# Rounding pieces of W_out earlier and reordering the end of an attention loop

## The chip, the cores and the metric

The kernel runs on one core of a Trainium2 chip. The metric is the device time of one execution, in microseconds (us). Five engines work side by side, each through its own list of instructions in order: TensorE (PE) multiplies and transposes, VectorE (DVE), ScalarE (ACT) and GpSimd (POOL) work elementwise, and SyncE (SP) issues DMAs. They wait for one another through semaphores only.

## The reference

Two layers of an encoder on 1024 tokens of 1024 features, in float32. Each layer mixes tokens with three kinds of heads (neighbourhood attention, a gated unit, a Fourier transform), normalises every head, multiplies by `w_out`, and then applies a SwiGLU block:

```
for l in range(DEPTH):                       # DEPTH = 2
    h = rms_norm(x, norm_mix_g[l])
    q, k, v, z_b, x_c = jnp.split(h @ w_in[l], splits, axis=-1)
    mix_a = neighbourhood_attention(q, k, v, rpb[l])
    mix_b = spatial_gating(z_b, ...)
    mix_c = fourier_mix(x_c)
    mix = head_rms_norm(jnp.concatenate([mix_a, mix_b, mix_c], axis=-1), head_norm_g[l])
    x = x + mix @ w_out[l]
    h = rms_norm(x, norm_ffn_g[l])
    x = x + (jax.nn.silu(h @ w_gate[l]) * (h @ w_up[l])) @ w_down[l]
return rms_norm(x, final_norm_g)
```

## The kernel before

Every float32 product is made of three products of rounded halves (`split3`, L1647): an operand is split into a rounded part "hi" (ACT, a copy to the rounded type) and the remainder "lo" (DVE or POOL, a subtraction), and hi*hi, hi*lo and lo*hi are summed in a PSUM bank. All activations are kept transposed, features on the 128 partitions.

The order of work is written out by hand on every engine, with `l` as the layer. What matters here is the attention loop and the stage after it.

The attention loop works through 8 tiles of 128 queries, each with 8 heads, two heads in each of 32 steps `i`. On PE a step is `scores(i)` (L1773, six matmuls on L1786), `values(i - 2)` (L1804, twelve on L1819), and two `turn_probs` (L1793, six transposes on L1800). DVE adds the bias and takes the maximum (L1243), ACT takes the exponent (`probs`, L864, L868), and the turned probabilities are copied from PSUM by DVE (L1253) for even heads and by ACT (L880) for odd ones. When a tile's values are done, DVE copies them to SBUF (`att_heads`, L1266), PE turns them to tokens (`turn_heads`, L1826, L1834), ACT squares (L892), DVE sums (L1281, L1285), POOL raises to the power -1/2 (L652), DVE multiplies (`att_tok`, L1290), PE turns them back (`turn_tokens`, L1837, L1841), and ACT copies them to `att_raw` (L897). The banks are shared: 6 and 7 take the turned tiles by parity, and in the first eight steps also the batches of the other heads (`turn_batch`, L1846), whose halves ACT (L887) and DVE (L1258) make. `turn_heads(0)` waits for the batch before last, since it takes over its bank.

The output product of the stage after the loop needs `w_out` in 16 pieces, numbered 18 to 33, each 128 x 1024. SP loads a piece (L435) as soon as its place in SBUF is free, ACT makes its hi part (`piece_hi`, L699, L702) and POOL its lo part (`piece_lo`, L620, L624). Where in its list ACT takes a piece is given by the step: 18 at step 14, 19 at 29, 20 at 33, 21 at 36. On POOL, piece 18 stands behind the power of tile 2, 19 behind that of tile 5, 20 behind that of tile 6, and the rest behind that of tile 7. Pieces 18, 19 and 20 belong to features of the other heads, whose input is ready long before, so PE begins the output product with them while the last tile is still on its way: `out_early(b)` (L1867) is 9 matmuls into bank b, three with each of the three pieces, and each bank waits until the attention loop is done with it. Between the eight `out_early` calls PE turns the last tiles. Pieces 21 to 25 follow in order, 24 matmuls each, and then the second half of the tokens with pieces 26 to 33.

Of the kernel before, what the change touches and what calls it, by code (L numbers as in the profile page):

```python
# [151 lines left out]
def build(nc, x, win, wout, wom, wg, wu, wd, bias, wsp, bsp, lng, lnb, gmix, ghead, gffn, gfin,  # L152
          tw, bd, ident, out):
    ctx = ExitStack()
    with ctx:
# [457 lines left out]
        @block.gpsimd  # L613
        def _(pool):
            nc.gpsimd.memset(ONES[:, :], 1.0).then_inc(memsets, 1)
            nc.gpsimd.memset(NHALF[:, :], -0.5).then_inc(memsets, 1)
            nc.gpsimd.memset(EPS_T[:, :], EPS).then_inc(memsets, 1)
            pool.wait_ge(memsets, 3)

            def piece_lo(l, p):  # L620

                s = ALL_SLOT[p]
                pool.wait_ge(w_hi, split_nth(l, p))
                nc.gpsimd.tensor_tensor(WL[s][:, :], WR[s][:, :], WH[s][:, :], ALU.subtract).then_inc(w_ready, 1)  # L624

            def ffn_rstd(n):

                pool.wait_ge(y_var, n)
                nc.gpsimd.tensor_tensor(RTF[:, :], RTF[:, :], NHALF[:, 0:4], ALU.pow).then_inc(y_rstd, 1)

            pool.wait_ge(w_ready, 1)
            piece_lo(0, 1)
            for l in range(DEPTH):
                piece_lo(l, 2)
                pool.wait_ge(rt_var, l + 1)
                nc.gpsimd.tensor_tensor(RT[:, :], RT[:, :], NHALF[:, 0:8], ALU.pow).then_inc(rt_made, 1)
                for p in (3, 4, 5, 6, 7, 8):
                    piece_lo(l, p)
                pool.wait_ge(ln_var, l + 1)
                nc.gpsimd.tensor_tensor(LR[:, :], LR[:, :], NHALF[:, 0:8], ALU.pow).then_inc(ln_rstd, 1)  # L640
                for p in (14, 15, 9, 10, 12, 11):
                    piece_lo(l, p)
                for n in range(2):
                    pool.wait_ge(hs_var, l * 2 + n + 1)
                    nc.gpsimd.tensor_tensor(SR[:, :], SS[:, :], NHALF[:, :], ALU.pow).then_inc(hs_rstd, 1)
                    if n == 0:
                        piece_lo(l, 13)
                for p in (17, 16):
                    piece_lo(l, p)
                for t in range(8):  # L650
                    pool.wait_ge(o_var, l * 8 + t + 1)
                    nc.gpsimd.tensor_tensor(SR[:, 0:HA], SS[:, 0:HA], NHALF[:, 0:HA], ALU.pow).then_inc(o_rstd, 1)  # L652
                    if t in (2, 5, 6):
                        piece_lo(l, {2: 18, 5: 19, 6: 20}[t])
                for p in range(21, 30):
                    piece_lo(l, p)
                ffn_rstd(2 * l + 1)
                for p in range(30, PIECES):
                    piece_lo(l, p)
                ffn_rstd(2 * l + 2)  # L660
                if l + 1 < DEPTH:
                    piece_lo(l + 1, 0)
                    pool.wait_ge(t_lo, (l + 1) * DN_STEPS)
                    piece_lo(l + 1, 1)
            for h in range(2):
                ffn_rstd(2 * DEPTH + h + 1)
# [3 lines left out]
        def _(act):  # L670
# [28 lines left out]
            def piece_hi(l, p):  # L699
                s = ALL_SLOT[p]  # L700
                act.wait_ge(w_landed[s], 16 * (l * PER_SLOT[s] + nth_in_slot(p) + 1))
                nc.scalar.activation(WH[s][:, :], WR[s][:, :], ACT.Copy).then_inc(w_hi, 1)  # L702
# [95 lines left out]
            for l in range(DEPTH):  # L798
# [73 lines left out]
                for i in range(41):  # L872
                    if i < 32:
                        probs(2 * i)
                    if 1 <= i < 33:
                        t = 2 * (i - 1) + 1
# [6 lines left out]
                    if i < 8:  # L883
                        b = BATCHES[i]
# [9 lines left out]
                    if i >= 12 and i % 4 == 0:  # L894
# [2 lines left out]
                        nc.scalar.activation(raw_out(tile),  # L897
                                             B[6 + tile % 2][:, :].rearrange("p (k r c) -> p k r c", k=NP, c=QC),
                                             ACT.Copy).then_inc(raw_made, 1)
                    if i in (14, 29, 33):  # L900
                        piece_hi(l, {14: 18, 29: 19, 33: 20}[i])
                    if i == 36:
                        mixed_hi(0)
                        piece_hi(l, 21)
                for p in range(22, 26):
                    piece_hi(l, p)
                mixed_hi(1)
                piece_hi(l, 26)
# [58 lines left out]
                for r in range(DN_STEPS):  # L967
# [8 lines left out]
                    i = r - 58  # L976
# [649 lines left out]
        def _(pe):  # L1626
# [26 lines left out]
            for l in range(DEPTH):  # L1653
# [9 lines left out]
                for k in range(KT_D):  # L1663
                    p = k // 4
# [219 lines left out]
                for i in range(33):  # L1884
                    if i < 32:
                        scores(i)
                    if i >= 2:
                        values(i - 2)
                    if i >= 10 and i % 4 == 2:
                        turn_tokens((i - 10) // 4)  # L1890
                    if i >= 1:
                        turn_probs(2 * (i - 1))
                        turn_probs(2 * (i - 1) + 1)
                    if i < 8:
                        turn_batch(i)
                    if i >= 7 and i % 4 == 3:
                        turn_heads((i - 7) // 4)
                pe.wait_ge(bt_lo, l * 8 + 8)
                out_early(0)
                values(31)  # L1900
                turn_tokens(6)
                out_early(1)
                turn_heads(7)
                for b in (2, 3, 4):
                    out_early(b)
                turn_tokens(7)
                for b in (6, 5, 7):
                    out_early(b)
# [195 lines left out]
```

## Time and profile before

| | us |
|---|---|
| median of 3 runs | 2129.43 |
| lowest and highest | 2127.15, 2131.02 |
| the profiled execution | 2130.46 |
| its span | 2128.7 |

| engine | busy us | share of the span |
|---|---|---|
| PE | 2077.0 | 98% |
| DVE | 1455.3 | 68% |
| ACT | 837.4 | 39% |
| POOL | 237.4 | 11% |

The span is the profiled stretch of that execution; 1.8 us lie around it. Busy times of an engine are summed over its instructions. The mean of the TensorE clock granted over the span was 0.994 of full speed.

### The profile page before, as it was taken

How to read it: one execution, taken by the hardware profiler on the slowest of the kernel's cores; microseconds unless marked ns; L12 is line 12 of the kernel's file. 1: busy time of each engine (PE TensorE's matmuls, PEld its weight loads, DVE VectorE, ACT ScalarE, POOL GpSimd, SP SyncE). 2: the span in 40 equal slices, each digit the busy share in tenths (PEclk: the TensorE clock that was granted, in tenths of full speed). 3: DMA queues.
4: the chain of work that ended last, by engine and by line, in shares of the span. 5: the costliest groups of instructions: out<-in, count | busy, mean ns of one | idle time of the engine just before them, and what ended most of it. 6: DMA issues, size and time to landing. Idle time of an engine off the chain costs nothing.

```text
span 2128.7 us, 27845 instructions
## 1 busy us (share of the span) xinstructions
PE 2077.0 (98%) x10352; PEld 1711.6 (80%) x10352; DVE 1455.3 (68%) x2355; ACT 837.4 (39%) x1476; POOL 237.4 (11%) x104
## 2 busy tenths in 40 slices
PE   7999999999999999999999999999999999999997
PEld 6888777887888888888888887787788888878886
DVE  6414684789877777787843237657997777777876
ACT  5221573453333323444622217634433332334442
POOL 2223024300000000000023300242000000000000
PEclk9999999999999999999999999999999999999998
DMA  5122343314333326633221314431253333384333
GB/s 182 60 89 70 119 120 109 99 45 157 116 102 102 104 99 227 222 98 96 85 78 60 97 43 139 140 131 38 69 173 103 101 104 99 114 285 131 96 97 114
DMA packets 104790, 240.21 MB, mean 113 GB/s; under 512 B 11088, under 2 KB 14032, under 8 KB 104400
## 3 DMA queue, kind: packets, MB, share of 16 engines
q1 hardware_dynamic: 92032, 211.16, 30.9%
q10 hardware_dynamic: 12624, 27.26, 3.6%
q8 instruction: 84, 1.38, 0.3%
q14 instruction: 50, 0.41, 0.1%
HBM read 188.58 MB, written 49.81 MB: 112 GB/s over the span
## 4 chain that ended last, share of the span: by engine, by line
PE 86%; DVE 7%; issue 3%; ACT 2%; DMA 1%; POOL 1%; DVEq 0%; POOLq 0%; SPq 0%; ACTq 0%
PE bank L1649 25%; PE bank L1651 25%; PE bank L1650 25%; PE bank L1819 2%; PE bank L1786 2%; PE bank L1800 2%; DVE s_lo L1083 1%; DVE t_lo L1332 1%; PE bank L1735 1%; DMA t_raw<-hidden_b 1%; DVE x_res L1300 1%; DVE y_sq_sum L1312 1%; PE bank L1737 0%; ACT y_sq L777 0%; PE bank L1841 0%
## 5 line engine op out<-in xcount | busy, mean ns | idle before, releaser
L1649 PE MATMUL bank<-t_hi,s_hi 128*128 128x512 f32 x1320 | 514.9, 390 | 10.3 <-DVE hid_g L1446 6.7
L1651 PE MATMUL bank<-t_hi,s_lo 128*128 128x512 f32 x1320 | 513.6, 389 | 0.0
L1650 PE MATMUL bank<-t_lo,s_hi 128*128 128x512 f32 x1320 | 513.6, 389 | 0.0
L1649 PEld LDWEIGHTS bank<-t_hi,s_hi 128*128 128x128 f32 x1320 | 247.8, 188 | 65.5 <-DVE hid_g L1446 9.2
L1651 PEld LDWEIGHTS bank<-t_hi,s_lo 128*128 128x128 f32 x1320 | 247.8, 188 | 51.4
L1650 PEld LDWEIGHTS bank<-t_lo,s_hi 128*128 128x128 f32 x1320 | 247.8, 188 | 51.3
L624 POOL TENSOR_TENSOR w_lo<-w_raw,w_hi 128x1024 fp32r<-128x1024 f32 x67 | 176.9, 2649 | 948.4 <-ACT w_hi L702 836.7
L1649 PE MATMUL bank<-h_hi,w_hi 128*128 128x512 f32 x512 | 202.1, 395 | 7.6 <-POOL w_lo L624 7.6
L1649 PE MATMUL bank<-b_hi,s_hi 128*128 128x512 f32 x528 | 206.6, 391 | 0.1
L1651 PE MATMUL bank<-b_hi,s_lo 128*128 128x512 f32 x528 | 206.2, 390 | 0.0
L1650 PE MATMUL bank<-b_lo,s_hi 128*128 128x512 f32 x528 | 206.0, 390 | 0.0
L1650 PE MATMUL bank<-h_lo,w_hi 128*128 128x512 f32 x512 | 200.2, 391 | 0.0
L1651 PE MATMUL bank<-h_hi,w_lo 128*128 128x512 f32 x512 | 200.2, 391 | 0.0
L734 ACT ACTIVATE s_hi<-w_u 128x512 fp32r<-128x512 f32 x146 | 92.2, 631 | 233.8 <-PE bank L1651 196.4
L734 ACT ACTIVATE s_hi<-w_down 128x512 fp32r<-128x512 f32 x154 | 97.2, 631 | 186.8 <-PE bank L1651 186.1
L1083 DVE TENSOR_TENSOR s_lo<-w_down,s_hi 128x512 fp32r<-128x512 f32 x154 | 107.4, 698 | 71.4 <-ACT s_hi L734 71.4
L734 ACT ACTIVATE s_hi<-w_g 128x512 fp32r<-128x512 f32 x146 | 92.0, 630 | 159.7 <-PE bank L1651 116.7
L1649 PE MATMUL bank<-w_hi,h_hi 128*128 128x512 f32 (+1 forms) x384 | 137.3, 358 | 13.5 <-DVE h_lo L1003 13.5
L1650 PE MATMUL bank<-w_lo,h_hi 128*128 128x512 f32 (+1 forms) x384 | 136.5, 356 | 0.0
L1651 PE MATMUL bank<-w_hi,h_lo 128*128 128x512 f32 (+1 forms) x384 | 136.5, 355 | 0.0
L702 ACT ACTIVATE w_hi<-w_raw 128x1024 fp32r<-128x1024 f32 x68 | 70.7, 1057 | 137.8 <-DMA w_raw<-in_win 116.7
L1649 PEld LDWEIGHTS bank<-h_hi,w_hi 128*128 128x128 f32 x512 | 96.6, 189 | 28.6 <-POOL w_lo L624 8.5
(196 smaller groups left out, 3274.7 us busy)
## 6 DMA issues: line engine op xcount, KB each, us to landing
w_g<-in_wg SPq DMA_DIRECT2D x44, 512.0 KB, 3.6
w_u<-in_wu SPq DMA_DIRECT2D x44, 512.0 KB, 4.4
t_raw<-hidden_t SPq DMA_DIRECT2D x88, 256.0 KB, 2.6
w_raw<-in_win SPq DMA_DIRECT2D x36, 512.0 KB, 4.0
bias<-in_bias SPq DMA_DIRECT2D x24, 768.0 KB, 5.6
t_raw<-hidden_b SPq DMA_DIRECT2D x66, 256.0 KB, 2.6
hidden_b<-hid_g SPq DMA_DIRECT2D x62, 256.0 KB, 2.0
hidden_t<-hid_x SPq DMA_DIRECT2D x44, 256.0 KB, 2.0
```

What stands on the lines that cost most here:

```text
L624: nc.gpsimd.tensor_tensor(WL[s][:, :], WR[s][:, :], WH[s][:, :], ALU.subtract).then_inc(w_ready, 1)
L702: nc.scalar.activation(WH[s][:, :], WR[s][:, :], ACT.Copy).then_inc(w_hi, 1)
L734: nc.scalar.activation(SH[q % W_RING][:, :], weight_block(q), ACT.Copy).then_inc(s_hi, 1)
L1083: nc.vector.tensor_tensor(SL[q % W_RING][:, :], weight_block(q), SH[q % W_RING][:, :], ALU.subtract)\
L1300: nc.vector.tensor_tensor(X[:, m, half(h)], B[m % 6 if h else m][:, :], X[:, m, half(h)], ALU.add).then_inc(out_added, 1)
L1312: nc.vector.tensor_tensor(ACCF[:, :], ACCF[:, :], SQF[i % 3][:, :], ALU.add)\
L1649: nc.tensor.matmul(bank, lh, rh, start=start, stop=False)
L1650: nc.tensor.matmul(bank, lh, rl, start=False, stop=False)
L1651: return nc.tensor.matmul(bank, ll, rh, start=False, stop=stop)
L1786: mm = nc.tensor.matmul(B[e][:, 0:NKEY].rearrange("p (r c) -> p r c", c=KC), qs[hp, c, q0:q0 + P], grid(ks[hp, c, :])[:, 4 * rr:4 * rr + K ...
L1800: mm = nc.tensor.transpose(B[2 + t % 2][:, n * P:(n + 1) * P], L[:, t % 4, n * P:(n + 1) * P], IDENT[:, :])
L1819: mm = nc.tensor.matmul(B[4 + tile % 2][e * DH:(e + 1) * DH, c * P:(c + 1) * P], VB[j % 2][:, rr + n, h * DH:(h + 1) * DH], PT[:, h % 4, n ...
```

## The change

In ACT's list, pieces 19 to 22 stand at steps 27, 30, 33 and 34 of the loop instead of 29, 33, 36 and behind the loop. In POOL's list, piece 19 stands behind the power of tile 4, 20 behind that of tile 5, and 21 and 22 behind that of tile 6. On PE, `turn_heads(0)` is issued in step 8 behind `scores(8)` instead of at the end of step 7, and of the first output products `out_early(1)` stands ahead of `turn_tokens(6)`, `out_early(2)` ahead of `turn_heads(7)`. SP's list is the same, and so is DVE's; no instruction is added or removed.

```
@@ gpsimd @@
                 for t in range(8):
                     pool.wait_ge(o_var, l * 8 + t + 1)
                     nc.gpsimd.tensor_tensor(SR[:, 0:HA], SS[:, 0:HA], NHALF[:, 0:HA], ALU.pow).then_inc(o_rstd, 1)
-                    if t in (2, 5, 6):
-                        piece_lo(l, {2: 18, 5: 19, 6: 20}[t])
-                for p in range(21, 30):
+                    if t in (2, 4, 5, 6):
+                        piece_lo(l, {2: 18, 4: 19, 5: 20, 6: 21}[t])
+                    if t == 6:
+                        piece_lo(l, 22)
+                for p in range(23, 30):
                     piece_lo(l, p)
@@ scalar @@
-                    if i in (14, 29, 33):
-                        piece_hi(l, {14: 18, 29: 19, 33: 20}[i])
+                    if i in (14, 27, 30, 33, 34):
+                        piece_hi(l, {14: 18, 27: 19, 30: 20, 33: 21, 34: 22}[i])
                     if i == 36:
                         mixed_hi(0)
-                        piece_hi(l, 21)
-                for p in range(22, 26):
+                for p in range(23, 26):
                     piece_hi(l, p)
@@ tensor @@
                     if i < 32:
                         scores(i)
+                    if i == 8:
+                        turn_heads(0)
                     if i >= 2:
                         values(i - 2)
...
-                    if i >= 7 and i % 4 == 3:
+                    if i >= 11 and i % 4 == 3:
                         turn_heads((i - 7) // 4)
                 pe.wait_ge(bt_lo, l * 8 + 8)
                 out_early(0)
                 values(31)
+                out_early(1)
                 turn_tokens(6)
-                out_early(1)
+                out_early(2)
                 turn_heads(7)
-                for b in (2, 3, 4):
-                    out_early(b)
+                out_early(3)
+                out_early(4)
                 turn_tokens(7)
                 for b in (6, 5, 7):
                     out_early(b)
```

On POOL, at the end of the attention loop (`head_rstd` is the power of a tile, `w_lo6`, `w_lo10`, `w_lo1` and `w_lo4` are the lo parts of pieces 19, 20, 21 and 22). Before:

```order
L652 TENSOR_TENSOR head_rstd_218<-head_ss_217,minus_half_215 128x8 x3
L624 TENSOR_TENSOR w_lo6_96<-w_raw6_108,w_hi6_84 128x1024
L652 TENSOR_TENSOR head_rstd_218<-head_ss_217,minus_half_215 128x8
L624 TENSOR_TENSOR w_lo10_100<-w_raw10_112,w_hi10_88 128x1024
L652 TENSOR_TENSOR head_rstd_218<-head_ss_217,minus_half_215 128x8
L624 TENSOR_TENSOR w_lo1_91<-w_raw1_103,w_hi1_79 128x1024
```

Now:

```order
L652 TENSOR_TENSOR head_rstd_218<-head_ss_217,minus_half_215 128x8 x2
L624 TENSOR_TENSOR w_lo6_96<-w_raw6_108,w_hi6_84 128x1024
L652 TENSOR_TENSOR head_rstd_218<-head_ss_217,minus_half_215 128x8
L624 TENSOR_TENSOR w_lo10_100<-w_raw10_112,w_hi10_88 128x1024
L652 TENSOR_TENSOR head_rstd_218<-head_ss_217,minus_half_215 128x8
L624 TENSOR_TENSOR w_lo1_91<-w_raw1_103,w_hi1_79 128x1024
L624 TENSOR_TENSOR w_lo4_94<-w_raw4_106,w_hi4_82 128x1024
L652 TENSOR_TENSOR head_rstd_218<-head_ss_217,minus_half_215 128x8
```

Piece 19 now stands ahead of the power of tile 5, piece 20 ahead of that of tile 6, and pieces 21 and 22 ahead of that of tile 7.

On ACT, from the square of tile 5 (L892, in step 27) on (`logits` are the exponents, `probs_t` the copies of turned probabilities). Before:

```order
L892 ACTIVATE bank5<-bank7 128x512
L868 ACTIVATE logits_75,exp_sum_221<-logits_75,minus_max_219 128x384
L880 ACTIVATE probs_t_207<-bank3 128x384
L868 ACTIVATE logits_75,exp_sum_221<-logits_75,minus_max_219 128x384
L897 ACTIVATE att_raw_58<-bank6 128x4x8x16
L868 ACTIVATE logits_75,exp_sum_221<-logits_75,minus_max_219 128x384
L880 ACTIVATE probs_t_207<-bank3 128x384
L868 ACTIVATE logits_75,exp_sum_221<-logits_75,minus_max_219 128x384
L702 ACTIVATE w_hi6_84<-w_raw6_108 128x1024
```

Now:

```order
L894 ACTIVATE bank5<-bank7 128x512
L704 ACTIVATE w_hi6_84<-w_raw6_108 128x1024
L870 ACTIVATE logits_75,exp_sum_221<-logits_75,minus_max_219 128x384
L882 ACTIVATE probs_t_207<-bank3 128x384
L870 ACTIVATE logits_75,exp_sum_221<-logits_75,minus_max_219 128x384
```

The hi part of piece 19 has moved ahead of four exponents, two copies and the copy of tile 4 to `att_raw`.

On PE, behind `values(31)`, the last values of the loop (its second six matmuls are the first row). Before:

```order
L1819 MATMUL bank5<-probs_t_207,v_band1_73 64x128 x6
L1841 MATMUL bank6<-ident_196,att_tok_76 128x128 x4
L1649 MATMUL bank1<-h_hi_50,w_hi7_85 128x512
L1650 MATMUL bank1<-h_lo_51,w_hi7_85 128x512
L1651 MATMUL bank1<-h_hi_50,w_lo7_97 128x512
```

Now:

```order
L1820 MATMUL bank5<-probs_t_207,v_band1_73 64x128 x6
L1650 MATMUL bank1<-h_hi_50,w_hi7_85 128x512
L1651 MATMUL bank1<-h_lo_51,w_hi7_85 128x512
L1652 MATMUL bank1<-h_hi_50,w_lo7_97 128x512
L1650 MATMUL bank1<-h_hi_50,w_hi6_84 128x512
L1651 MATMUL bank1<-h_lo_51,w_hi6_84 128x512
L1652 MATMUL bank1<-h_hi_50,w_lo6_96 128x512
L1650 MATMUL bank1<-h_hi_50,w_hi10_88 128x512
L1651 MATMUL bank1<-h_lo_51,w_hi10_88 128x512
L1652 MATMUL bank1<-h_hi_50,w_lo10_100 128x512
L1842 MATMUL bank6<-ident_196,att_tok_76 128x128 x4
```

The nine products into bank 1 have moved ahead of `turn_tokens(6)`.

## Rows read from the trace of the kernel before

**Rows 1.** Waits of PE, whole span: us in total, times, longest.
```profile
PE bank L1649 <- POOL w_lo L624: 7.6, 2, 3.8
PE bank L1834 <- DVE h_lo L1258: 1.3, 2, 0.6
```

**Rows 2.** Timeline of PE, layer 0, loop's end: start, us, engine, line [idle before].
```profile
324.17 0.88 PE L1819 MATMUL bank<-probs_t,v_band 128*64 128x128 f32 x12 [0.24 <-ACT probs_t L880]
...
325.61 0.47 PE L1649 MATMUL bank<-h_hi,w_hi 128*128 128x512 f32 x1
...
331.06 0.74 PE L1649 MATMUL bank<-h_hi,w_hi 128*128 128x512 f32 x1 [3.82 <-POOL w_lo L624]
...
332.58 1.55 PE L1819 MATMUL bank<-probs_t,v_band 128*64 128x128 f32 x12
...
336.84 0.60 PE L1834 MATMUL bank<-ident,att_heads 128*128 128x128 f32 x4
...
343.45 0.60 PE L1841 MATMUL bank<-ident,att_tok 128*128 128x128 f32 x4
...
350.04 0.39 PE L1649 MATMUL bank<-h_hi,w_hi 128*128 128x512 f32 x1
```

**Rows 3.** Timeline of PE, layer 1, the same place.
```profile
1370.84 0.47 PE L1649 MATMUL bank<-h_hi,w_hi 128*128 128x512 f32 x1
...
1396.57 0.39 PE L1649 MATMUL bank<-h_hi,w_hi 128*128 128x512 f32 x1
```

**Rows 4.** Busy time by stretch, PE: stretch, length, busy (x), clock, DMA share, GB/s.
```profile
332.50:334.70 2.20, 2.20 (x18) 0.53 0.00 0
...
1476.00:1478.00 2.00, 2.00 (x6) 0.50 0.00 0
```

**Rows 5.** Timeline of POOL, layer 0, loop's end.
```profile
317.22 1.64 POOL L652 TENSOR_TENSOR head_rstd<-head_ss,minus_half 128x8 f32<-128x8 f32 x1 [8.63 <-DVE head_ss L1285]
320.49 2.37 POOL L624 TENSOR_TENSOR w_lo<-w_raw,w_hi 128x1024 fp32r<-128x1024 f32 x1 [1.64 <-ACT w_hi L702]
327.07 1.64 POOL L652 TENSOR_TENSOR head_rstd<-head_ss,minus_half 128x8 f32<-128x8 f32 x1 [4.20 <-DVE head_ss L1285]
328.67 2.34 POOL L624 TENSOR_TENSOR w_lo<-w_raw,w_hi 128x1024 fp32r<-128x1024 f32 x1
```

**Rows 6.** Timeline of ACT, layer 0: square of tile 5, hi part of piece 19.
```profile
314.24 0.58 ACT L892 ACTIVATE bank<-bank 128x512 f32<-128x512 f32 x1
...
319.37 1.04 ACT L702 ACTIVATE w_hi<-w_raw 128x1024 fp32r<-128x1024 f32 x1
```

**Rows 7.** Timeline of DVE, layer 0: tile 5's sum, tiles 5 and 7 multiplied.
```profile
316.97 0.17 DVE L1285 SCALAR_TENSOR_TENSOR head_ss<-head_ss,exp_sum_sq 128x8 f32<-128x8 f32 x1
...
318.88 0.69 DVE L1290 TENSOR_TENSOR att_tok<-bank,head_rstd 128x512 f32<-128x512 f32 x1 [0.18 <-POOL head_rstd L652]
...
340.80 0.69 DVE L1290 TENSOR_TENSOR att_tok<-bank,head_rstd 128x512 f32<-128x512 f32 x1 [1.75 <-POOL head_rstd L652]
```

**Rows 8.** Timeline of PE, layer 0, steps 7 to 10 of the loop.
```profile
260.98 0.63 PE L1834 MATMUL bank<-ident,att_heads 128*128 128x128 f32 x4 [0.64 <-DVE h_lo L1258]
...
266.91 0.45 PE L1786 MATMUL bank<-k_hi,q_hi 64*128 64x384 f32 x2 [0.60 <-DVE minus_max L1243]
```

**Rows 9.** DMA issues, us to landing: piece 19 (at 307.33), pieces 21 to 23 (from 323.16).
```profile
w_raw<-in_wout SPq DMA_DIRECT2D x1, 512.0 KB, 3.5
...
w_raw<-in_wout SPq DMA_DIRECT2D x3, 512.0 KB, 4.7
```

**Rows 10.** DVE's sum of squares beside a piece on POOL; all 24 (ns min/median/max).
```profile
414.69 1.52 DVE L1312 TENSOR_TENSOR y_sq_sum<-y_sq_sum,y_sq 128x512 f32<-128x512 f32 x1 [0.70 <-ACT y_sq L777]
...
412.80 2.85 POOL L624 TENSOR_TENSOR w_lo<-w_raw,w_hi 128x1024 fp32r<-128x1024 f32 x1 [0.56 <-ACT w_hi L702]
...
L1312 DVE TENSOR_TENSOR y_sq_sum<-y_sq_sum,y_sq x24: 691/693/1948, 376.7 to 1472.4; 128x512 f32<-128x512 f32 x24
```

**Rows 11.** Timeline of PE, layer 1, first step of the gate and up products.
```profile
1473.22 1.02 PE L1636 MATMUL bank<-ones,y_sq_sum 128*128 128x1 f32 x8 [1.12 <-issue]
```

## The prediction

> **What bounds the kernel now.** PE is busy for 98% of the span, so time can only come from PE's waits and from stretches where its clock is low. I read the list of PE's waits first. Two of its rows belong to places that the change touches [rows 1]: 7.6 us in two waits of 3.8 us, one in each layer, for the lo part of a piece of W_out, and 1.3 us in two waits of 0.6 us for a batch of the other heads. Then I read the timelines of both places, and for the first one POOL's, ACT's and DVE's too.
>
> The long wait stands inside `out_early(0)`. PE begins it at 325.61, does six of its nine matmuls, and waits 3.82 us for piece 20 [rows 2]. POOL shows why: it makes the power of tile 6 from 327.07 and only then takes piece 20, from 328.67 for 2.34 us, which ends at 331.01, 0.05 us before PE goes on [rows 5]. The wait costs more than itself. The twelve matmuls of `values(31)` behind it take 1.55 us against 0.88 us in the loop [rows 2], at a granted clock of 0.53 [rows 4], that is mostly at the lower of its two levels, 1.2 GHz, after PE stood still. In layer 1 the wait is as long [rows 1], and the whole stretch lasts 1.3 us longer [rows 2, 3].
>
> **The end of the loop, what goes.** I measure the stretch from the first matmul of `out_early(0)` to the first one with piece 21. It is 350.04 - 325.61 = 24.43 us in layer 0 [rows 2] and 1396.57 - 1370.84 = 25.73 us in layer 1 [rows 3]. The work in it is 8 x 9 = 72 matmuls, `values(31)` and three turns. At full clock a turn and 27 matmuls took 343.45 - 336.84 = 6.61 us and 350.04 - 343.45 = 6.59 us [rows 2]. With 0.44 us for a turn (an estimate: its row begins 0.35 us ahead of the next one, and the first matmul behind it costs 0.09 us more) a matmul is 0.228 us. The other 18 matmuls are 4.1 us, the third turn 0.44, and `values(31)` 0.81 as in the loop, with some 0.1 for the seams: 6.6 + 6.6 + 5.5 = 18.7 us without any wait.
>
> What is late next? Piece 20's lo part now stands behind the power of tile 5. Its hi part comes in step 30, near 323, so its lo part ends near 326 (2.34 us later), before PE's seventh matmul at 325.61 + 1.4. `turn_tokens(6)` needs tile 6 multiplied by DVE, near 329.5 (power at 327.07 for 1.64, then 0.69); with `out_early(1)` ahead of it PE gets there at 325.61 + 5.1 = 330.7. `turn_heads(7)` needs that turn and a copy of 0.7 us, and `out_early(2)` covers it with 2.1 us. `turn_tokens(7)` needs tile 7 through ACT, DVE, POOL and DVE again: from the start of `turn_heads(7)` at 336.84 to the end of the multiplication at 340.80 + 0.69 = 341.49 this took 4.65 us [rows 2, 7]. PE has its turn and 18 matmuls to do meanwhile, 4.55 us. So about 0.15 us of wait is left there, if POOL is free for the power. It is: pieces 21 and 22 are issued at 323.16 and land some 4 to 5 us later [rows 9], their lo parts follow the power of tile 6 at 328.7 and end near 333.4, and the power of tile 7 is asked for at 335.5. The new stretch is 18.7 + 0.15 = 18.9 us in each layer. The gain is 24.43 - 18.88 = 5.55 and 25.73 - 18.88 = 6.85, together **12.4 us**.
>
> **The head of the loop.** `turn_heads(0)` waits 0.64 us at the end of step 7 [rows 8]. Behind `scores(8)`, which needs nothing that is late, that wait is covered. DVE gets the scores of step 8 earlier by the turn as well. In step 10 PE waits 0.60 us for DVE's maximum [rows 8], so DVE sets the pace there. It did not start on step 8 until PE gave it scores, so its chain moves earlier too, and the gain isn't taken back. I work out 0.75 us in each layer, between 0 (if DVE's pace swallowed it) and 1.0: **1.5 us** in both.
>
> **What the earlier rounding costs.** ACT. The hi part of piece 19 (1.04 us) now follows the square of tile 5, at 314.24 + 0.5 = 314.74 [rows 6]. The copy behind it moves by about 0.3 us and `values(27)` by 0.2 us. The same happens in step 30 with piece 20, and there PE already waits 0.24 us for ACT's copy [rows 2]; it will wait 0.2 us more.
>
> POOL is worse. The lo part of piece 19 runs from 315.86 for 2.34 us, to 318.20. The power of tile 5 began at 317.22 [rows 5] and stands behind it now: 0.98 us later. DVE's multiplication at 318.88 waited for that power already [rows 7], so it is late by as much. Behind it on DVE stand the maxima of step 30, on PE `turn_tokens(5)`. PE loses some 0.8 us there, 1.0 us with the 0.2 us of step 30.
>
> There may be more. DVE's L1285 at 316.97 [rows 7], which makes the input of that power, falls into the time of piece 19's lo part. It reads two operands from SBUF. Rows that bound this: in the loop DVE's operations beside piece 19 (from 320.49 [rows 5]) kept their lengths, the maxima among them, which gives 1.0 us; but a sum of two operands in SBUF took 1.52 us instead of 0.69 when it began at 414.69, in the middle of a piece on POOL that lasted to 415.65 [rows 10], as if held until it was over. Held in the same way, L1285 ends at 318.4, and the two maxima behind it, the power and the multiplication move by 1.2 us: 1.4 us with the 0.2. L1285 is of the second kind, so I take 1.4 us in each layer: **-2.8 us**, against -2.0 at the other end.
>
> The Trainium skill, SBUF — State Buffer, section "Who interferes with whom", says that a DVE instruction with two SBUF inputs contends with a GpSimd instruction that reads SBUF, and that the one issued first keeps the shared ports for the whole instruction. By that rule L1285 is held, and the sum is the one with -2.8; without it, it would be 0.8 us lower.
>
> **The sum.** -12.4 - 1.5 + 2.8 = -11.1 us. The profiled execution's 2130.46 becomes 2119.3. It lies 1.0 us above the median of 2129.43, so for a median I take **2118.3 us**.
>
> The pieces that ACT and POOL no longer make behind the loop cost nothing there: PE is at full work from 350.04 on, and pieces 23 to 25 are ready ahead of it as before.
>
> **Rivals.**
> 1. The low clock is not the wait's doing and stays. Then only the waits go: 7.6 + 1.3 - 2.8 = 6.1 us, 2123.3. Against it: the clock is full in the loop on both sides. 0.05.
> 2. The new pauses in the loop, or one at `turn_tokens(7)`, are longer or bring the clock down. Layer 1 shows the price: behind a pause of 1.12 us [rows 11] the clock was 0.50 [rows 4], and ten matmuls took some 2 us more. One such fall in one or both layers gives 2120.3 to 2122.3. The pause at `turn_tokens(5)` is about 1 us long. 0.15.
> 3. The wait moves whole. Something else (the power of tile 6 behind a late piece 20) holds PE as long as before: 2129. It needs piece 20 some 4 us later than I have it. 0.05.
> 4. Slower. ACT's list stops at step 27 because piece 19 has not landed, and exponents, copies and everything behind them stop with it. It is issued at 307.33 and lands 3.5 us later [rows 9], at 310.8; ACT wants it at 314.74. From a landing 3.9 us later than that each further us costs one in each layer, and 5.6 us more would undo the gain: landing 13 us after issue gives 2129, beyond it slower, 2134 at 15.5. No landing here took over 6 us. 0.03.
>
> **How the numbers follow.** My forecast has 0.72. What spreads it: the stage of the second half's sums, where layer 1 had the pause of 1.12 us and the low clock [rows 4, 11] and layer 0 next to no pause. The time at which pieces on POOL meet sums on DVE decides that, and all of this moves. Both layers or neither could have it, 2.9 us up or down: 2115.4 to 2121.2, and the three runs themselves spread by 3.9 us. The range 2114.0 to 2122.5 holds this and rival 2; rivals 1, 3 and 4 (0.13) stay outside. A measurement of this kernel can tell 0.2% (4.3 us) from no change. Forecast and rivals 1 and 2 are faster by more: 0.92; rival 3 is the same: 0.05; rival 4 slower: 0.03.
>
> **What would show it.** No wait for `w_lo` in `out_early(0)`, and the stretch to the first matmul with piece 21 is 18.9 us in both layers at full clock. `turn_heads(0)` without a wait. The power of tile 5 about 1.0 to 1.3 us later against its square, a pause of PE for `att_tok` in step 30 that isn't there now, and L1285 of tile 5 stretched to over 1 us if it is held. I am wrong if that pause is long enough to bring the clock down, or if a wait for `att_tok` of more than 1 us appears in the stretch.

## The result and the profile after

The changed kernel took 2119.09 us (median of 4 runs, 2118.17 to 2119.63), the kernel before 2128.95 in the same set. The ratio is 0.9943, 95% interval 0.9932 to 0.9955: faster by 9.9 us, about 0.6%. The profiled execution took 2119.24 us with a span of 2117.4, against 2130.46 and 2128.7.

The first view is again the list of PE's waits, whole span: what was waited for, us in total, times, longest.

```profile
PE bank L1650 <- DVE h_lo L1004: 13.0, 1, 13.0
PE bank L1650 <- DVE hid_g L1447: 6.5, 6, 1.5
...
PE bank L1787 <- DVE minus_max L1244: 3.7, 6, 0.7
PE bank L1650 <- DVE hid_ag L1447: 3.4, 2, 1.7
PE bank L1637 <- issue: 2.2, 2, 1.1
...
PE bank L1820 <- ACT probs_t L882: 1.2, 4, 0.4
```

Both rows of [rows 1] are gone: no wait for `w_lo`, none for `h_lo` in the loop (the 13.0 us of the first row stand at the start of the program; before, they were 13.5). Lines are one or two higher than before. The timeline of PE, layer 0, at the loop's end shows the place of [rows 2].

```profile
315.73 0.88 PE L1820 MATMUL bank<-probs_t,v_band 128*64 128x128 f32 x12 [0.19 <-ACT probs_t L882]
...
318.10 0.45 PE L1787 MATMUL bank<-k_hi,q_hi 64*128 64x384 f32 x2 [0.68 <-DVE minus_max L1244]
...
324.13 0.88 PE L1820 MATMUL bank<-probs_t,v_band 128*64 128x128 f32 x12 [0.39 <-ACT probs_t L882]
...
325.57 0.48 PE L1650 MATMUL bank<-h_hi,w_hi 128*128 128x512 f32 x1
...
327.83 0.88 PE L1820 MATMUL bank<-probs_t,v_band 128*64 128x128 f32 x12
...
338.05 0.66 PE L1842 MATMUL bank<-ident,att_tok 128*128 128x128 f32 x4
...
344.69 0.39 PE L1650 MATMUL bank<-h_hi,w_hi 128*128 128x512 f32 x1
```

From 325.57 to 344.69 no row carries a wait, and `values(31)` takes 0.88 us, as in the loop, where it took 1.55 at the lower clock. The stretch is 344.69 - 325.57 = 19.12 us, against 24.43. In layer 1 it is the same 19.12 (1368.20 to 1387.32), against 25.73 [rows 2, 3]. The clock was full in it: the row of PE's busy time by stretch (length, busy, granted clock) reads

```profile
325.00:345.00 20.00, 20.00 (x105) 1.00 0.33 120
```

The price of the earlier rounding stands in the first and second row above, at 315.73 and 318.10. Around them, on ACT, POOL and DVE, in order of time:

```profile
313.58 1.04 ACT L704 ACTIVATE w_hi<-w_raw 128x1024 fp32r<-128x1024 f32 x1
314.69 2.37 POOL L624 TENSOR_TENSOR w_lo<-w_raw,w_hi 128x1024 fp32r<-128x1024 f32 x1 [7.29 <-ACT w_hi L704]
315.79 1.30 DVE L1286 SCALAR_TENSOR_TENSOR head_ss<-head_ss,exp_sum_sq 128x8 f32<-128x8 f32 x1
317.17 1.64 POOL L652 TENSOR_TENSOR head_rstd<-head_ss,minus_half 128x8 f32<-128x8 f32 x1
318.84 0.69 DVE L1291 TENSOR_TENSOR att_tok<-bank,head_rstd 128x512 f32<-128x512 f32 x1 [0.32 <-POOL head_rstd L652]
...
323.09 2.36 POOL L624 TENSOR_TENSOR w_lo<-w_raw,w_hi 128x1024 fp32r<-128x1024 f32 x1 [4.29 <-ACT w_hi L704]
323.48 1.99 DVE L1277 SCALAR_TENSOR_TENSOR exp_sum_sq<-exp_sum 128x8 f32<-128x8 f32 x1
```

Piece 19's lo part runs from 314.69 to 317.06. The sum of eight columns on L1286 begins at 315.79 and ends at 317.09, when POOL is done: 1.30 us instead of 0.17 [rows 7]. The maxima of step 30 stand behind it on DVE, and PE waits 0.68 us for them at `scores(30)`. L1277 at 323.48 is held beside piece 20 in the same way and nobody waits for it.

I split the time with four marks in each layer: s0, the first scores matmul of the loop; s10, the one of step 10; E, the first matmul of `out_early(0)`; F, the first one with piece 21. They are read from PE's timeline of each kernel (layer 0 / layer 1, us):

| kernel | s0 to s10 | s10 to E | E to F |
|---|---|---|---|
| before | 27.56 / 27.56 | 58.70 / 58.70 | 24.43 / 25.73 |
| changed | 26.87 / 26.87 | 59.83 / 59.82 | 19.12 / 19.12 |
| e1, PE's order only | 26.88 / 26.86 | 58.69 / 58.69 | 25.79 / 25.59 |
| e2, rounding only | 27.57 / 27.54 | 59.84 / 59.83 | 19.64 / 19.64 |
| e3 | 26.88 / 26.87 | 59.10 / 59.07 | 19.13 / 19.14 |
| e4 | 26.88 / 26.87 | 59.65 / 59.67 | 19.08 / 19.13 |
| e5, changed again | 26.88 / 26.86 | 59.81 / 59.85 | 19.14 / 19.13 |
| e6 | 26.88 / 26.87 | 59.45 / 59.47 | 19.14 / 19.12 |

Where the clock is full and the lists of the stretch are the same, they repeat to 0.05 us from kernel to kernel, while the whole runs of one kernel spread by 1.5 to 7. The experiments are judged by them first, though each kernel has one traced execution only. For the change they give 5.31 + 6.61 = 11.92 us at the end of the loop, 0.69 + 0.69 = 1.38 at its head and -1.13 - 1.12 = -2.25 within it, together 11.05 us. The span fell by 11.3. The rest is a balance of parts outside these stretches: PE's new pause in layer 0 cost 0.9 us (below), and 1.05 us were gained elsewhere, 0.5 of them ahead of the first loop (s0 of layer 0 stands at 238.87 instead of 239.35). That stretch alone varied from 238.9 to 239.8 us over the thirteen traces, so these 1.05 us are not shown to be the change's.

### The profile page after: what moved, and what is told of

It reads as the page before. It is cut to its first block, busy times and chain, and to the rows that moved or that the text cites. A ratio compares the mean times of both kernels' runs of the same rounds, so it can differ in the third digit from the quotient of the medians.

```text
span 2117.4 us, 27845 instructions
## 1 busy us (share of the span) xinstructions
PE 2072.6 (98%) x10352; PEld 1709.4 (81%) x10352; DVE 1454.9 (69%) x2355; ACT 836.9 (40%) x1476; POOL 234.7 (11%) x104
## 3 DMA queue, kind: packets, MB, share of 16 engines
q8 instruction: 84, 1.38, 0.3%
## 4 chain that ended last, share of the span: by engine, by line
PE 86%; DVE 7%; issue 3%; ACT 2%; DMA 1%; POOL 0%; DVEq 0%; POOLq 0%; SPq 0%; ACTq 0%
PE bank L1650 25%; PE bank L1651 25%; PE bank L1652 25%; PE bank L1820 2%; PE bank L1787 2%; PE bank L1801 2%; DVE s_lo L1084 1%; DVE t_lo L1333 1%; PE bank L1736 1%; DMA t_raw<-hidden_b 1%; DVE x_res L1301 1%; DVE y_sq_sum L1313 1%; PE bank L1738 0%; ACT y_sq L779 0%; PE bank L1842 0%
## 5 line engine op out<-in xcount | busy, mean ns | idle before, releaser
L1650 PEld LDWEIGHTS bank<-b_hi,s_hi 128*128 128x128 f32 x528 | 99.5, 188 | 21.4 <-issue 0.9
```

What stands on the lines that cost most here:

```text
L1650: nc.tensor.matmul(bank, lh, rh, start=start, stop=False)
```

## The experiments

Two theories of where the time comes from. A: the rounding takes away the wait and the fall of the clock behind it, the new order on PE covers the chain of the last tiles, and the price in the loop is POOL's queue plus one DVE sum held beside a piece. B: the order of PE's calls does the work, or the price is POOL's queue alone.

### One half at a time

**e1**: the new order on PE, with the rounding of before.

```
+                    if i == 8:
+                        turn_heads(0)
...
-                    if i >= 7 and i % 4 == 3:
+                    if i >= 11 and i % 4 == 3:
...
-                turn_tokens(6)
                 out_early(1)
+                turn_tokens(6)
+                out_early(2)
                 turn_heads(7)
-                for b in (2, 3, 4):
-                    out_early(b)
+                out_early(3)
+                out_early(4)
```

> The changed order on PE (turn of tile 0 behind the scores of step 8, output products of banks 1 and 2 ahead of the turns) with the old rounding on ACT and POOL. Theory (the gain of 10 us comes from piece 20 no longer being late, the PE order only keeps a later wait away): PE waits 3.8 us for the lo part of piece 20 in each layer as before, the clock falls behind it as before, and only the turn of tile 0 brings 0.68 us in each layer: 1.4 us below the kernel before, about 2127.5. Rival (the order of the output products carries half of the gain or more): 2124 or less.

Measured: 2129.61 us, ratio 0.9991 (0.9981 to 1.0001) with 10 runs: not told apart from the kernel before, which took 2132.05 in the same set (I expected 2127.5). PE's waits, PE's timeline at the place, and its busy time by stretch:

```profile
PE bank L1649 <- POOL w_lo L624: 7.7, 2, 3.8
```

```profile
330.21 0.79 PE L1649 MATMUL bank<-h_hi,w_hi 128*128 128x512 f32 x1 [3.82 <-POOL w_lo L624]
```

```profile
332.00:334.00 2.00, 2.00 (x14) 0.50 0.00 0
```

The wait and the fall of the clock stand as before; only the head of the loop gained its 0.69 us per layer. Layer 0's stretch is even 1.4 us longer, 25.8 as in layer 1. What makes 24.4 or 25.8 of it is how long the clock stays low: in the kernel before, layer 0 was at full clock again where layer 1, as long after its wait, was not.

```profile
335.00:337.00 2.00, 2.00 (x11) 1.00 0.69 244
...
1380.00:1382.00 2.00, 2.00 (x8) 0.50 0.66 199
```

**e2**: the rounding of the change, with PE's order of before.

```
-                    if t in (2, 5, 6):
-                        piece_lo(l, {2: 18, 5: 19, 6: 20}[t])
-                for p in range(21, 30):
+                    if t in (2, 4, 5, 6):
+                        piece_lo(l, {2: 18, 4: 19, 5: 20, 6: 21}[t])
+                    if t == 6:
+                        piece_lo(l, 22)
+                for p in range(23, 30):
...
-                    if i in (14, 29, 33):
-                        piece_hi(l, {14: 18, 29: 19, 33: 20}[i])
+                    if i in (14, 27, 30, 33, 34):
+                        piece_hi(l, {14: 18, 27: 19, 30: 20, 33: 21, 34: 22}[i])
...
```

> The changed rounding on ACT and POOL with the old order on PE. Theory: no wait for piece 20 and no low clock, but the turn of tile 6 stands right behind the last values and PE reaches it some 0.8 us before DVE has multiplied tile 6; with 0.7 us in each layer for the turn of tile 0 that is 2.5 to 3 us above the changed kernel: 2121.5 to 2122. Rival (the order on PE does nothing): 1.4 us above the changed kernel, 2120.5, the turn of tile 0 alone. If a pause of 0.8 us brought the clock down, 2124 or more.

Measured: 2121.56 us, ratio 0.9954 (0.9936 to 0.9971). PE's waits:

```profile
PE bank L1842 <- DVE att_tok L1291: 1.5, 2, 0.8
PE bank L1835 <- DVE h_lo L1259: 1.3, 2, 0.6
```

The wait for the piece is gone, and tile 6 is what comes late next: PE waits 0.74 us for it at `turn_tokens(6)`. The stretch is 19.64 us, 0.5 longer than with both halves. So of the 11.9 us at the loop's end 10.9 come from the rounding and 1.0 from PE's order on top of it (alone, the order gave nothing there, e1); the 1.4 at the head come from PE's order, and the whole price in the loop (59.84 against 58.70) from the rounding.

### What the price in the loop is made of

**e3**: ACT as changed; on POOL, piece 19 behind the power of tile 5, with piece 20, and pieces 21 and 22 behind that of tile 6.

```
-                    if t in (2, 4, 5, 6):
-                        piece_lo(l, {2: 18, 4: 19, 5: 20, 6: 21}[t])
-                    if t == 6:
-                        piece_lo(l, 22)
+                    if t in (2, 5, 6):
+                        piece_lo(l, {2: 18, 5: 19, 6: 21}[t])
+                    if t in (5, 6):
+                        piece_lo(l, {5: 20, 6: 22}[t])
```

> The changed kernel, but the lo part of piece 19 stands behind the power of tile 5 on POOL again (with piece 20 behind it); ACT's list is the changed one. Theory (of the 1.13 us that each layer's loop loses, some 0.7 us come from POOL's piece, which holds the sum of tile 5 on DVE and stands ahead of its power, and 0.4 us from ACT): the sum of tile 5 takes 0.17 us instead of 1.30, PE has no wait of 0.68 us for the maxima in step 30, and the time is 1.4 us below the changed kernel: 2117.7. Rival (ACT's earlier pieces are the cost): the loop still loses 1.1 us, 2119.1.

Measured: 2119.25 us, ratio 0.9936 (0.9918 to 0.9955). DVE and POOL in layer 0:

```profile
316.71 0.17 DVE L1286 SCALAR_TENSOR_TENSOR head_ss<-head_ss,exp_sum_sq 128x8 f32<-128x8 f32 x1
316.95 1.64 POOL L652 TENSOR_TENSOR head_rstd<-head_ss,minus_half 128x8 f32<-128x8 f32 x1 [8.64 <-DVE head_ss L1286]
318.55 2.37 POOL L624 TENSOR_TENSOR w_lo<-w_raw,w_hi 128x1024 fp32r<-128x1024 f32 x1
```

With no piece beside it the sum takes 0.17 us and PE's wait of 0.68 us is gone. Steps 10 to E are 59.1 us: 0.73 less than changed, 0.39 above before. The 0.39 is ACT's part, since ACT's list is that of the change. The stretch behind stays 19.1, so piece 19 needn't come before the power of tile 5 at all. The median is 1.5 us above the 2117.7 that I expected; the marks came as expected, and where the gain went in the profiled execution is shown further down, beside e9.

**e4**: POOL and ACT as changed, but tile 5's reduced sums stay in their PSUM bank, so that L1286 (here L1287) reads one operand from SBUF instead of two. The bank is then handed to PE one operation later.

```
+                        ss = B[5][:, 0:HA] if tile == 5 else SS[:, 0:HA]
-                        nc.vector.tensor_reduce(SS[:, 0:HA], ...
+                        nc.vector.tensor_reduce(ss, ...
...
-                        nc.vector.scalar_tensor_tensor(out=SS[:, 0:HA], in0=SS[:, 0:HA], scalar=1.0 / DH,
+                        nc.vector.scalar_tensor_tensor(out=SS[:, 0:HA], in0=ss, scalar=1.0 / DH,
...
-                            pe.wait_ge(o_red, l * 8 + tile - 1)
+                            pe.wait_ge(o_var if tile == 7 else o_red, l * 8 + tile - 1)
```

> The changed kernel, but the sum of squares of tile 5 stays in PSUM, so that the operation behind it on DVE reads one operand from PSUM and one from SBUF instead of two from SBUF; POOL's and ACT's lists are the changed ones. Theory A (a piece on POOL holds a DVE operation with two SBUF inputs): this operation takes 0.2 us instead of 1.30 beside the same piece; the power is still behind the piece, so the multiplication is as late, and the loop loses some 0.7 to 1.0 us instead of 1.13: 2118.3 to 2119. Rival B (it isn't the operands: anything small on DVE stops beside the piece): the operation still takes 1.3 us and the time is 2119.1.

Measured: 2120.21 us, ratio 0.9944 (0.9929 to 0.9960). POOL, DVE and PE in layer 0:

```profile
314.76 2.38 POOL L624 TENSOR_TENSOR w_lo<-w_raw,w_hi 128x1024 fp32r<-128x1024 f32 x1 [7.29 <-ACT w_hi L704]
...
315.87 0.17 DVE L1287 SCALAR_TENSOR_TENSOR head_ss<-bank,exp_sum_sq 128x8 f32<-128x8 f32 x1
...
317.10 1.64 POOL L652 TENSOR_TENSOR head_rstd<-head_ss,minus_half 128x8 f32<-128x8 f32 x1
...
319.52 0.66 PE L1843 MATMUL bank<-ident,att_tok 128*128 128x128 f32 x4 [0.50 <-DVE att_tok L1292]
```

The same operation at the same moment beside the same piece takes 0.17 us once one of its two inputs comes from PSUM. In layer 1 it is the same (0.17 us). So the hold is by the second SBUF input. The power still stands behind the piece until 317.10, and PE now waits 0.50 us at `turn_tokens(5)`. The loop took 59.66 against 59.82: of the 1.13 us per layer, 0.39 is ACT, 0.57 POOL's queue (59.66 - 59.09), and 0.17 the hold. The median, 2120.21, is above the 2118.3 to 2119 that I expected, while the loop's loss against before, 0.96 us, lies within the expected 0.7 to 1.0. The queue and the hold overlap: with the sum held, the power lost nothing more by the piece.

**e6**: the POOL order of e3, and ACT's hi part of piece 19 in step 28 instead of 27. **e5** is the changed kernel once more, on the same chip.

```
-                    if i in (14, 27, 30, 33, 34):
-                        piece_hi(l, {14: 18, 27: 19, 30: 20, 33: 21, 34: 22}[i])
+                    if i in (14, 28, 30, 33, 34):
+                        piece_hi(l, {14: 18, 28: 19, 30: 20, 33: 21, 34: 22}[i])
```

> The changed kernel once more, beside the next three on one chip, since the size of a gain of 1 or 2 us is read against it. Expected: 2119 us, 9 to 12 us below the kernel before. The loop from the wait in step 10 to the first output product takes 59.8 us (58.7 before), the stretch behind it 19.1 us.

> The changed kernel with both lo parts of pieces 19 and 20 behind the power of tile 5 on POOL, and the hi part of piece 19 at step 28 instead of 27 on ACT, where it doesn't follow a square but a copy to att_raw. Theory (the loop loses 0.57 us to POOL's piece ahead of the power, 0.17 us to the held sum and 0.19 us to each hi part that stands in front of a copy): 0.74 us less for the loop of each layer from POOL, up to 0.2 us more or less from ACT: 59.0 to 59.3 us from the wait in step 10 to the first output product, 1.0 to 1.8 us below the changed kernel over both layers. Rival (step 28 on ACT is as full as step 27, and PE's copy is later by more): 59.5 us or more, no gain.

Measured: e5 2119.04 us, ratio 0.9954 (0.9942 to 0.9967), e6 2118.00, ratio 0.9947 (0.9933 to 0.9960). From step 10 to E e6 took 59.46, 0.37 less than changed and 0.37 more than e3: above the 59.0 to 59.3 expected, and what the rival said of ACT. Its timeline of PE in layer 0 shows why it is the worse place:

```profile
319.30 0.88 PE L1820 MATMUL bank<-probs_t,v_band 128*64 128x128 f32 x12 [0.54 <-issue]
```

The hi part at 317.17 holds back ACT's copy of the turned probabilities in that step, and PE stands 0.54 us ahead of `values(28)`. Of the two steps, 27 is the cheaper one for ACT. The 1.0 us between the medians of e5 and e6 is inside their intervals.

### A pause that couldn't be saved alone

After the change PE still stops for 1.1 us at the token sums of the feedforward stage, in both layers ([rows 11] had one; before, layer 0 had 0.19). They need DVE's last sum of squares. Whether layer 0 has the pause is the outcome of a race that a few tenths of a us decide. DVE and POOL in layer 0 of e5, which has the pause:

```profile
406.00 5.04 DVE L1333 TENSOR_TENSOR b_lo<-t_lo_raw,b_hi 128x512 fp32r<-128x512 f32 x2
408.05 2.44 POOL L624 TENSOR_TENSOR w_lo<-w_raw,w_hi 128x1024 fp32r<-128x1024 f32 x1 [0.37 <-ACT w_hi L704]
```

and of e9 (below), whose lists are those of e5 up to here:

```profile
405.32 2.84 DVE L1333 TENSOR_TENSOR b_lo<-t_lo_raw,b_hi 128x512 fp32r<-128x512 f32 x2
407.55 2.89 POOL L624 TENSOR_TENSOR w_lo<-w_raw,w_hi 128x1024 fp32r<-128x1024 f32 x1 [0.53 <-ACT w_hi L704]
```

L1333 reads two operands from SBUF. Its second operation begins 81.8 us behind E in both. In e5 POOL's piece had begun at 81.68, and DVE stood until it was over; in e9 the piece began at 81.86, behind it, and only the next sum of squares was held (1.52 us). The last sum then begins 94.1 us behind E instead of 94.95. POOL waits there for ACT's hi part, and ACT for the piece to land. In layer 0 POOL came first in the changed kernel, e2, e4, e5, e7 and e10, DVE in e3, e6, e8, e9 and e11; in layer 1 POOL did in all of them. So that e3 and e6 wait only 0.18 us in layer 0 can't be put down to their edits.

**e7** issues both the sums and the spread of their reciprocal roots two blocks (six matmuls, 1.38 us) later. **e8** is e7 with the rounding of e6.

```
-                        if q == 0 and k == 3:
+                        if q == 1 and k == 1:
                             ...
                             token_sums(B[6], ACCF, y_ssq)
-                        if q == 1 and k == 3:
+                        if q == 2 and k == 1:
                             spread_rstd(B[6], 2 * l + 2)
```

> The changed kernel with the token sums of the second half and the spreading of their result put six matmuls later on PE (steps 1 and 2 of the gate and up products instead of 0 and 1). Theory (PE stands still for 1.1 us at these sums in both layers, and in one of them the clock falls behind it, which costs 2 us more): no pause and no low clock there, 2.2 us for the pauses and 2 us for the clock: 2115, and no wait for anything else behind it. Rival (the wait only moves to the spreading or to the first operands of the second half): 2118 to 2119.

> The two edits before this one together. If each does what it should, their gains add, since they lie in different stages: 1.5 us from the loop and 2.2 to 4 us from the sums, 2113 to 2115. If the clock falls somewhere else for the pause that is gone, 2116 to 2117.

Measured: e7 2118.89 us, ratio 0.9952 (0.9939 to 0.9964), which is e5's; e8 2118.04, ratio 0.9945 (0.9933 to 0.9958), which is e6's. Both missed the 2115 and 2113 to 2115 expected, and e7 came out as its rival had it. The pause is gone, and nothing came of it. Layer 1 of e7, sums, spread, DVE's next step, and the first product of the second half of the feedforward:

```profile
1463.06 0.95 PE L1637 MATMUL bank<-ones,y_sq_sum 128*128 128x1 f32 x8
...
1466.73 1.05 PE L1644 MATMUL bank<-ident,rstd_tok_ffn 128*128 128x128 f32 x8
1467.88 1.41 DVE L1325 SCALAR_TENSOR_TENSOR t_lo_raw<-x_res,g_ffn,bank 128x512 f32<-128x512 f32 x2 [1.93 <-PE bank L1644]
...
1513.69 0.79 PE L1650 MATMUL bank<-t_hi,s_hi 128*128 128x512 f32 x1 [3.03 <-DVE hid_ag L1447]
```

and the same place in the changed kernel:

```profile
1463.95 1.02 PE L1637 MATMUL bank<-ones,y_sq_sum 128*128 128x1 f32 x8 [1.11 <-issue]
...
1467.68 1.05 PE L1644 MATMUL bank<-ident,rstd_tok_ffn 128*128 128x128 f32 x8
1468.83 1.41 DVE L1325 SCALAR_TENSOR_TENSOR t_lo_raw<-x_res,g_ffn,bank 128x512 f32<-128x512 f32 x2 [1.18 <-PE bank L1644]
...
1514.64 0.50 PE L1650 MATMUL bank<-t_hi,s_hi 128*128 128x512 f32 x1 [1.67 <-DVE hid_ag L1447]
```

From DVE's L1325 to the product it is 45.81 us in both. PE came 1.4 us sooner and waited 3.03 us instead of 1.67: the wait moved whole. The spread had stayed where it was against the work before it, so L1325 had too. Three more runs took sums and spread apart. **e9** is the changed kernel with the sums alone later (the first two lines of the diff of e7). **e10** leaves the sums and puts the spread two blocks sooner. **e11** is e9 with the rounding of e6.

```
-                        if q == 1 and k == 3:
+                        if q == 1 and k == 1:
                             spread_rstd(B[6], 2 * l + 2)
```

> As e7_sums_two_blocks_later (the token sums at q 1, k 1), but the spread of the reciprocal roots back at q 1, k 3, where the changed kernel has it. My theory: the feedforward stage is paced by a chain that begins with DVE's L1325 and ends at the first matmul of t_hi; in e7 and in the changed kernel alike L1325 began 45.82 us ahead of that matmul. e7 took PE's pause of 1.1 us away but the spread, and so L1325, stayed where it was, 100.6 us behind the first output product, and PE gave the time back in its wait for hid_ag, 3.04 us instead of 1.67. With the spread two blocks (1.38 us) sooner L1325 begins 99.3 us behind the first output product, the wait for hid_ag is back at 1.7 us, and the distance from the first output product to the first matmul of t_hi falls from 146.4 to 145.1 us: 1.3 us per layer, and no fall of the clock at hid_ag (1.6 us each), if the length of that wait brings it. The median falls by 2.6 us against the changed kernel to 2116.5, or by more against e7. Rival: the pace is set by something else (the weights of the feedforward, or DVE's own work before it), and the first matmul of t_hi stays 146.4 us behind the first output product with a longer wait: 2119.

> The changed kernel with the token sums where they are (q 0, k 3, with PE's pause of 1.1 us) and the spread two blocks sooner, at q 1, k 1. By the theory of the chain from L1325 this gives as much as e9: L1325 1.3 us sooner, the distance from the first output product to the first matmul of t_hi 145.1 us, with the pause of 1.1 us still there and a wait for hid_ag of only 0.4 us; 2116.5. If PE's own work and its pause set the pace, the pause stays, the wait for hid_ag stays at 1.67 us and the median at 2119.

> e9 and the rounding of e6 (hi part of piece 19 in step 28, lo parts of pieces 19 and 20 behind the power of tile 5) in one. If both are worth what I think, 0.4 us per layer from the loop (60 to 59.45 us from step 10 to the first output product) and 1.3 us per layer from the chain: 2115.7, the fastest of all. If the chain is not what paces it, 2118.0 as e6 and e8.

Measured: e9 2118.25 us, ratio 0.9940 (0.9926 to 0.9953); e10 2120.39, ratio 0.9951 (0.9939 to 0.9964); e11 2115.44 (2114.32 to 2117.81), ratio 0.9931 (0.9919 to 0.9944). By the marks, in layer 1, where none of these four had a low clock between E and the product:

| kernel | pause at the sums | L1325 to product | wait at the product | E to product |
|---|---|---|---|---|
| changed | 1.11 | 45.81 | 1.67 | 146.44 |
| e7 | none | 45.81 | 3.03 | 146.48 |
| e10 | 1.07 | 46.83 | 1.32 | 146.17 |
| e9 | none | 45.81 | 1.67 | 145.21 |

e9 gained 1.2 of the 1.3 us that I gave it, in both layers (145.23 in layer 0). e10 missed: I expected it to gain as much, and it gained 0.3, with a median no better than e5's. Its trace shows where the rest went. From L1325 to the product it took 46.83 us instead of 45.81, and the 1.0 us stands in one place, 14 us behind L1325. ACT and DVE of e10 there, and DVE of e9 at the same operation:

```profile
1480.87 0.60 ACT L951 ACTIVATE hid_au<-bank 128x512 f32<-128x512 f32 x1 [0.91 <-PE bank L1652]
1482.02 0.69 DVE L1084 TENSOR_TENSOR s_lo<-w_early,s_hi 128x512 fp32r<-128x512 f32 x1 [1.34 <-ACT s_hi L736]
```

```profile
1479.67 0.69 DVE L1084 TENSOR_TENSOR s_lo<-w_early,s_hi 128x512 fp32r<-128x512 f32 x1 [0.31 <-ACT s_hi L736]
```

In e10 ACT waits 0.91 us for PE's bank, makes DVE's next input behind it, and DVE stands 1.34 us instead of 0.31. So two paths of nearly one length meet, PE's own work and DVE's chain from L1325, and they meet through ACT, well ahead of the product. e7 shortened PE's, e10 DVE's, e9 both.

e9's median is 1.7 us above the 2116.5 expected. Its trace names what ate that in the profiled execution, which was the median one: the clock fell in layer 0 behind a wait that the changed kernel has too. PE's timeline of e9 and its busy time by stretch, and then both of e5:

```profile
846.45 0.67 PE L1650 MATMUL bank<-t_hi,s_hi 128*128 128x512 f32 x1 [1.79 <-DVE hid_g L1447]
```

```profile
848.00:850.00 2.00, 2.00 (x6) 0.50 1.05 398
```

```profile
848.36 0.50 PE L1650 MATMUL bank<-t_hi,s_hi 128*128 128x512 f32 x1 [1.74 <-DVE hid_g L1447]
```

```profile
850.00:852.00 2.00, 2.00 (x11) 1.00 1.04 399
```

From the product in layer 0 to s0 of layer 1 it is 809.61 us in e9 against 808.06 in e5. e3 lost more at the same place: it waited 2.37 us at 847.49, the clock fell behind that too, and the distance is 810.34. This is what its expected gain went into.

e11 is the fastest median of all, at what I expected (2115.7), 15.2 us below the kernel before on its chip. Against the changed kernel it stands by the ratios, 0.9931 to 0.9943 and 0.9954; its interval (0.9919 to 0.9944) overlaps with the first one's (0.9932 to 0.9955) and touches the second's, and the two weren't timed side by side, so by times alone it is not shown to be the faster one. The marks (0.37 us in the loop and 1.22 behind it, per layer) say that some 3 us of it come from the edits. e3's place for the hi part (step 27) would give another 0.37 us per layer by the marks; that wasn't run.

## Why the prediction was right

The forecast was 2118.3 us, 2119.3 for a profiled execution; measured were 2119.09 and 2119.24. The mechanism was right; that the number is this close is partly luck. The forecast took 0.5 us too much for the loop's end and 0.55 too much for the price in the loop, and these cancel, and so nearly do the new pause in layer 0 (0.9 us) and the 1.05 us from parts that the sum doesn't name. Step by step:

- **The end of the loop**: 12.4 us forecast, 11.92 measured. The stretch is 19.12 us, not 18.88, without one wait in it: the 0.15 us of wait for tile 7 did not come, and the bare work was put 0.4 us too short. The rest was right as put: the wait of 3.8 us, the low clock behind it and 1.3 us more in layer 1 went together, and e1 shows that they stay without the rounding (rival 1 and rival 3 fall).
- **The head**: 1.5 forecast, 1.38 measured, all from PE's order (e1). The wait of 0.60 us in step 10 stayed, and DVE did not take the gain back.
- **The price in the loop**: 2.8 us forecast, 2.25 measured; the other end was 2.0. The held sum was right in kind: 1.30 us against the forecast "over 1 us". Counted from step 10, which now begins 1.17 us sooner, DVE's multiplication of tile 5 came 1.13 us later than before (318.84 + 1.17 against 318.88), forecast 1.2. What was sized too high is what PE loses by that delay: the sum took 1.2 us per layer, and the changed kernel lost 0.74 more than e3, where the delay is missing. ACT's part was sized too low, 0.2 against the 0.39 of e3. The place of the pause was wrong: PE waited for the maxima at `scores(30)`, which stand behind the sum on DVE, and not for `att_tok`. That pause came only when e4 took the hold away.
- **ACT**: 0.2 + 0.2 us forecast, 0.19 more at 315.73 and 0.39 against 0.24 at 324.13; e3 puts its sum at 0.39 in the loop. The forecast's total had counted only one of its two 0.2.
- **The spread**: I left open in which layers PE stops before the token sums and in which the clock falls. In the profiled execution both layers stop now, by the race shown above, and the fall moved from layer 1 to layer 0. From the sums to the first product of the second half it was 50.67 us in layer 0 before and 52.28 after, and 52.29 and 50.69 in layer 1, so the two moves cancel but for 0.9 us of new pause in layer 0. Rival 2's price (2 us for a fall) was a little high here: 1.6.

The Trainium skill, SBUF — State Buffer, section "Who interferes with whom", gave the hold by the second SBUF input. The trace agrees with it, and e4 is the direct test: 1.30 us with two such inputs, 0.17 with one. What it could not give is the cost, since the hold overlaps the piece's own place in the queue: 0.17 us of 1.13 (e4 against changed).

## What to carry to other kernels

A wait of PE can cost more than itself, by the low clock behind it: two waits of 3.8 us were worth 4.8 and 6.1 by the rounding alone (e2), though a new wait of 0.74 us stood there. Look for such a wait first, and move the work that releases it before work that isn't due. When a long piece on POOL is moved ahead of a short one, read which DVE operations with two SBUF inputs fall into it, and what is queued behind them on DVE: the cheapest place for the piece is behind the power, not ahead of it (e3). Here a pause was worth its length only when the other engines' chain to the same next meeting point was shortened too: find that point and measure both paths to it (e7, e10 and e9).

## What the runs showed of the hardware

A wait of one length brings the clock down in one execution and not in another: behind 1.11 to 1.13 us before the token sums the clock fell in layer 0 of the changed kernel and stayed full in layer 1. PE's busy time by stretch in the changed kernel, one row of layer 0 and two of layer 1:

```profile
424.00:426.00 2.00, 2.00 (x6) 0.50 0.00 0
...
1464.00:1466.00 2.00, 2.00 (x13) 1.00 0.00 0
1466.00:1468.00 2.00, 2.00 (x12) 1.00 0.00 0
```

e5, the same program, had that pause in both layers (1.07 and 1.13 us) and no fall in either; its span was 2117.2 against 2117.4. What a fall costs depends on what stands behind it. From E to the product it was 148.04 us with one (layer 0, changed) and 146.42 without (layer 0, e5): 1.6 us. Behind the four waits of 3.0 us at the product (e7 and e8, both layers) the clock fell each time, and nothing was lost by it: from there to s0 of layer 1 it was 808.21 and 807.80 us, against 808.06 in e5 with no fall. PE's next two waits took it up; in layer 1 they were 0.59 and 1.28 us in the changed kernel, and in e7 the first is gone and the second 0.44.

Some of the spread between runs of one kernel may be which of its waits of 1 to 2 us catches a fall; with one traced execution of each kernel, and two of the changed one, that isn't shown. A gain of 1 us per layer is judged by marks in the trace before it is judged by medians.
